# One group of memory values computed right behind the memory keys, the adaptive weights spread over 30 units, and the second norm moved into a 16-unit stage

## The reference

```python
def memory_cross_attention(hn, mem_n, w_q, w_k, w_v, w_o):
    q = (hn @ w_q).reshape(b, s, XA_HEADS, XA_HEAD_DIM)
    k = (mem_n @ w_k).reshape(b, m, XA_HEADS, XA_HEAD_DIM)
    v = (mem_n @ w_v).reshape(b, m, XA_HEADS, XA_HEAD_DIM)
    ...
```

## Time and profile before

| | us |
|---|---|
| median of 3 runs | 3084.89 (3084.48 to 3085.43) |
| time of the profiled execution | 3085.91 |
| its span, first to last instruction | 3084.1 |
| PE busy | 3028.6 |
| DVE busy | 2146.0 |
| ACT busy | 1581.2 |

### The profile page before, as it was taken

The page is one execution under the profiler, slowest core; times in us unless marked ns, Lnnn a source line. Parts: engine busy times, 40 slices in busy tenths (PEclk is TensorE's granted clock), DMA queues, the critical chain, the costliest instruction groups (busy, mean ns, idle before and its releaser), DMA issues.

```text
span 3084.1 us, 44830 instructions
## 1 busy us (share of the span) xinstructions
PE 3028.6 (98%) x16750; PEld 2593.7 (84%) x16750; DVE 2146.0 (70%) x2720; ACT 1581.2 (51%) x1948; POOL 52.2 (2%) x52
## 2 busy tenths in 40 slices
PE   7899999999999999999999999999999999999998
PEld 5688878888788887888888888888888888888887
DVE  3389888788588787647668855566567777777554
ACT  3355444556544566444556654445345555555443
POOL 0032000000000000000000000000000000000000
PEclk9999999999999999999999999999999999999999
DMA  9966848786578656545555555575355555555554
GB/s 392 371 244 232 306 179 314 282 320 228 187 264 294 227 186 219 196 164 197 172 192 168 182 189 191 181 243 197 130 171 178 191 190 190 190 189 188 189 191 143
DMA packets 181403, 667.46 MB, mean 216 GB/s; under 512 B 20212, under 2 KB 20604, under 8 KB 179708
## 3 DMA queue, kind: packets, MB, share of 16 engines
q1 hardware_dynamic: 179580, 661.13, 62.2%
q10 hardware_dynamic: 1664, 4.19, 0.4%
HBM read 658.95 MB, written 6.30 MB: 216 GB/s over the span
## 4 chain that ended last, share of the span: by engine, by line
PE 84%; DVE 8%; DMA 4%; ACT 2%; DVEq 1%; issue 1%; SPq 0%; ACTq 0%
PE acc L791 45%; PE acc L795 22%; PE acc L802 4%; PE acc L804 4%; PE acc L803 4%; DVE w_lo L2060 3%; DMA mod_raw<-in_w_mod 2%; DVE mod_raw L2071 1%; DMA ada_more<-in_w_ada 1%; ACT w_hi L1314 1%; PE msc L839 1%; DMA raw<-in_w_xa_k 1%; PE acc L778 0%; PE msc L1210 0%; PE msc L1230 0%
## 5 line engine op out<-in xcount | busy, mean ns | idle before, releaser
L2060 DVE TENSOR_TENSOR w_lo<-raw,w_hi 128x1024 fp32r<-128x1024 f32 x1020 | 1241.3, 1227 | 597.7 <-ACT w_hi L1314 587.0
L1314 ACT CAST w_hi<-raw 128x1024 fp32r<-128x1024 f32 x1020 | 1061.3, 1048 | 835.6 <-PE acc L795 572.4
L791 PE MATMUL acc<-a_pair,w_hi 128*128 128x512 f32 x2944 | 929.7, 397 | 2.8 <-DVE w_lo L2060 1.6
L795 PEld LDWEIGHTS acc<-a_pair,w_lo 128*128 128x128 f32 x2944 | 553.0, 188 | 130.6
L791 PE MATMUL acc<-b_pair,w_hi 128*128 128x512 f32 x1792 | 569.9, 399 | 18.1 <-DVE w_lo L2060 18.1
L795 PE MATMUL acc<-a_pair,w_lo 128*128 128x256 f32 x2944 | 578.6, 278 | 0.0
L791 PEld LDWEIGHTS acc<-a_pair,w_hi 128*128 128x128 f32 x2944 | 450.3, 189 | 5.1 <-issue 1.9
L791 PE MATMUL acc<-f_pair,w_hi 128*128 128x512 f32 x1408 | 442.4, 395 | 0.0
L795 PEld LDWEIGHTS acc<-b_pair,w_lo 128*128 128x128 f32 x1792 | 337.2, 188 | 79.8
L795 PE MATMUL acc<-b_pair,w_lo 128*128 128x256 f32 x1792 | 352.8, 278 | 0.0
L795 PEld LDWEIGHTS acc<-f_pair,w_lo 128*128 128x128 f32 x1408 | 264.5, 188 | 62.5
(11 more groups left out here) (369 smaller groups left out, 2497.9 us busy)
## 6 DMA issues: line engine op xcount, KB each, us to landing
raw<-in_w_ffn_up SPq DMA_DIRECT2D x176, 512.0 KB, 4.0
mod_raw<-in_w_mod SPq DMA_DIRECT2D x128, 512.0 KB, 5.0
raw<-in_w_ffn_down SPq DMA_DIRECT2D x88, 512.0 KB, 3.3
ada_more<-in_w_ada SPq DMA_DIRECT2D x40, 512.0 KB, 14.2
raw<-in_w_xa_k SPq DMA_DIRECT2D x32, 512.0 KB, 12.6
raw<-in_w_k SPq DMA_DIRECT2D x32, 512.0 KB, 4.5
raw<-in_w_v SPq DMA_DIRECT2D x32, 512.0 KB, 5.6
raw<-in_w_even_out SPq DMA_DIRECT2D x32, 512.0 KB, 4.6
```

Source lines behind the costliest of these rows:

```text
L791: pe.matmul(acc[:, bank(stage, g) + m, :], w_h[:, cols], pair[:, :, kc, :], start=begin, stop=False, skip_group_check=True)
L795: mm = pe.matmul(acc[:, bank(stage, g) + m, 0:T], w_l[:, cols], pair[:, 0, kc, :], start=False, stop=end, skip_group_check=True)
L1314: nc.scalar.copy(w_hi[:, slot], source).then_inc(hi_done, 1)
L2060: vec.tensor_tensor(w_lo[:, slot], source, w_hi[:, slot].bitcast(F32), ALU.subtract).then_inc(lo_done, 1)
```

## The change

It makes the first quarter of the memory's values (8 T units) right behind the keys, so 40 units instead of 32 stand ahead of the context's keys. The modulation's quads are spread over 30 units. The context's load goes behind the last of them, and the context's pair is made at units 33 to 40, one chunk a unit. The second quarter takes the place beside the first norm (same size as before). The stage beside the second norm shrinks from 24 to 16 units, with the norm's steps at earlier units. It also changes some places: `masked` and the scores in `lat_q`, the broadcast load of `top` in two halves, the sums in `even_out`, ACT's step in `SGU_HIGH_AT`; and the second product of a retention head covers only the 128 columns that are read.

```diff
-ADA_OVER = 24
+ADA_OVER = 30
...
     Stage("mem_k", "w_xa_k", "F", 1, groups=4, dve=1),
+    Stage("mem_va", "w_xa_v", "T", 1, groups=1),
     Stage("ctx_k", "w_k", "F", 1, gate=True, act=1, dve=1),
...
     Stage("even_out", "w_even_out", "F", 1, groups=4, act=2, dve=2),
-    Stage("mem_va", "w_xa_v", "T", 1, groups=1),
+    Stage("mem_vb", "w_xa_v", "T", 1, groups=1, first_unit=DC // KU),
     Stage("sgu_v", "w_sgu_v", "T", 1, groups=4, act=1, woven=True),
...
     Stage("odd_out", "w_odd_out", "F", 1, groups=4, act=2, dve=2),
-    Stage("mem_vb", "w_xa_v", "T", 1, groups=3, first_unit=DC // KU),
+    Stage("mem_vc", "w_xa_v", "T", 1, groups=2, first_unit=2 * DC // KU),
     Stage("ret_q", "w_ret_q", "F", 1, act=1, dve=1, woven=True),
...
-          "mlstm_z": spread(16, 14), "pool_z": spread(16, 11), "even_out": range(0, 24, 2), ...
+          "mlstm_z": spread(16, 14), "pool_z": spread(16, 11), "even_out": spread(20, 12), ...
...
-CTX_AT = STAGE["mem_k"].n - 5
-CTX_STEPS = {CTX_AT: (0,), CTX_AT + 1: (1, 2), CTX_AT + 2: (3,), CTX_AT + 3: (4, 5), CTX_AT + 4: (6,)}
-MOD_TURN = CTX_AT - 2
+CTX_AT = STAGE["mem_k"].n + 1
+CTX_STEPS = {CTX_AT + q: (q,) for q in range(7)}
+MOD_TURN = CTX_AT - 1
...
-SGU_HIGH_AT = {at + 1: q for at, q in SGU_NORM_AT.items() if q < 8}
+SGU_HIGH_AT = {at + (1 if q < 2 else 2): q for at, q in SGU_NORM_AT.items() if q < 8}
 SGU_X_AT = {24 + c: c for c in range(DC)}
-MIX_SUMS_AT = 17
-MIX_NORM_AT = 18
-NORMALISE_AT = {4: 0, 6: 1, 8: 2, 10: 3}
-SQUARES_AT = {5: 0, 7: 1, 9: 2, 11: 3}
-MIX_X_AT = {6: 0, 8: 1, 10: 2, 12: 3}
-QUARTERS_AT = {7: 0, 9: 1, 11: 2, 13: 3}
+MIX_SUMS_AT = 12
+MIX_NORM_AT = 13
+NORMALISE_AT = {4: 0, 5: 1, 7: 2, 9: 3}
+SQUARES_AT = {5: 0, 6: 1, 8: 2, 10: 3}
+MIX_X_AT = {7: 0, 9: 1, 11: 2, 13: 3}
+QUARTERS_AT = {6: 0, 8: 1, 10: 2, 11: 3}
...
-SCORES_AT = 13
-MASKED_AT = 14
+SCORES_AT = 12
+MASKED_AT = 11
...
                 def load_key(j):
                     g, k = stage.kinds[j][1:3]
-                    if j == CTX_LOAD_AT:
-
-                        sp.wait_ge(pe_step, BEFORE["mem_norm"]["pe"] + 1)
-                        nc.sync.dma_start(x[:], t["ctx"]).then_inc(ctx_in, 16)
...
+                sp.wait_ge(pe_step, BEFORE["mem_norm"]["pe"] + 1)
+                nc.sync.dma_start(x[:], t["ctx"]).then_inc(ctx_in, 16)
...
-                        if stage.name == "lat_q" and j == 6:
+                        if stage.name == "lat_q" and j in (6, 8):
 
                             sp.wait_ge(top_out, 16)
-                            nc.sync.dma_start(top[:].rearrange("p d h t -> p (d h t)"),
-                                              t["top"].rearrange("d h t -> (d h t)").partition_broadcast(P)).then_inc(top_in, 16)
+                            d = (j - 6) // 2
+                            nc.sync.dma_start(top[:, d].rearrange("p h t -> p (h t)"),
+                                              t["top"][d].rearrange("h t -> (h t)").partition_broadcast(P)).then_inc(top_in, 16)
...
             run("mem_k", b_pair, 0, batch=2, side=mem_sums)
+            run("mem_va", b_pair, PAIR["mem"])
...
-            run("mem_va", a_pair, PAIR["mem_va"], side=first_norm)
+            run("mem_vb", a_pair, PAIR["mem_vb"], side=first_norm)
...
-            run("mem_vb", b_pair, PAIR["mem_vb"], side=second_norm)
-            run("ret_q", a_pair, PAIR["mem_vb"], batch=2)
+            run("mem_vc", b_pair, PAIR["mem_vc"], side=second_norm)
+            run("ret_q", a_pair, PAIR["mem_vc"], batch=2)
...
-                            mm = pe.matmul(msc[:, h % 2, k * T:(k + 1) * T], kf[:, h, k * P:(k + 1) * P], qf[:, h, :],
+                            mm = pe.matmul(msc[:, h % 2, k * T + k * P:(k + 1) * T], kf[:, h, k * P:(k + 1) * P], qf[:, h, k * P:T],
...
             run("mem_k", store_keys, side=mem_chunks)
+            run("mem_va", store_values("mem_va"), side=lambda j: mem_chunks(STAGE["mem_k"].n + j))
...
             run("mem_k", none(), side=mem_chunks, dest=keys_out, scale=token_scale)
+            run("mem_va", none(), side=lambda j: mem_chunks(STAGE["mem_k"].n + j))
```

More of the change, by code:

```diff
@@ L195 @@
           "lat_q": (0, 2, 4, 5, 7, 8, 10, 11, 13), "lat_o": spread(16, 12), "pool_u": spread(16, 9),
-          "mlstm_z": spread(16, 14), "pool_z": spread(16, 11), "even_out": range(0, 24, 2), "sgu_u": spread(32, 18), "sgu_z": spread(26, 14)}
+          "mlstm_z": spread(16, 14), "pool_z": spread(16, 11), "even_out": spread(20, 12), "sgu_u": spread(32, 18), "sgu_z": spread(26, 14)}
 MOD_PLACE = {}
@@ L219 @@
 assert max(MOD_ROWS_AT) < MOD_TURN
-KV_GROUP = {"mem_k": 0, "mem_va": 4, "mem_vb": 5}
+KV_GROUP = {"mem_k": 0, "mem_va": 4, "mem_vb": 5, "mem_vc": 6}
 MEM_AT = [12 + 2 * q for q in range(8)]
@@ L302, in rg_root_step @@
     return rg_act_step(4 * q + 5, 2) + 1 if q < 3 else rg_act_step(DC - 1, 2) + 1
-PAIR = dict(mem=8, ctx=16, lat=24, even_out=28, mem_va=36, sgu=44, odd_out=48, mem_vb=56, mix=64, ret_proj=68, rnn_proj=72,
+PAIR = dict(mem=8, ctx=16, lat=24, even_out=28, mem_vb=36, sgu=44, odd_out=48, mem_vc=56, mix=64, ret_proj=68, rnn_proj=72,
             mix_out=76, xa=84, xa_o=88, ffn=96, ffn_down=107)
@@ L1062, in row_sums @@
                     steps.done(mm)
-            run("sgu_v", b_pair, PAIR["mem_va"], batch=2, side=row_sums)
+            run("sgu_v", b_pair, PAIR["mem_vb"], batch=2, side=row_sums)
             def mix(j):
@@ L1543, in conv_silu, with values, group @@
                 return group
[L1545 to L1552, removed]
+            def values(name):
+                def group(i, g):
+                    first = bank(STAGE[name], g)
+                    for tt in range(2):
+                        mm = nc.scalar.activation(va[:, tt, 2 * g:2 * g + 2, 0:MLSTM_D],
+                                                  acc[:, first + tt, :].rearrange("p (h n) -> p h n", h=2), ACT.Copy, scale=0.5)
+                    mm.then_inc(acc_free, 1)
+                    act.drain()
+                    ran(act.nop())
+                return group
             def wide_and_last(j):
@@ L1589, in key_tokens @@
                     high(j - 9, 1)
-            run("ctx_v", values, side=key_tokens)
+            run("ctx_v", values("ctx_v"), side=key_tokens)
             def first_states(j):
@@ L1616, in exps @@
                     steps.end("lat_gates")
-            run("lat_v", values, side=exps)
+            run("lat_v", values("lat_v"), side=exps)
             def mlstm_exps(r):
@@ L1660, in output_gate @@
             def output_gate(i, g):
-                nc.scalar.activation(both, acc[:, 2 * (g % 2):2 * (g % 2) + 2, :].rearrange("p a b -> p (a b)"), ACT.Tanh,
+                first = bank(STAGE["lat_o"], g)
+                nc.scalar.activation(both, acc[:, first:first + 2, :].rearrange("p a b -> p (a b)"), ACT.Tanh,
                                      scale=0.5).then_inc(acc_free, 1)
@@ L1769, in row_sums @@
             def row_sums(j):
-                sgu_chunks(STAGE["mem_va"].n + j)
+                sgu_chunks(STAGE["mem_vb"].n + j)
                 if j == ROW_SUM_AT:
@@ L1775, in row_sums @@
                                               msc[:, 0:2, :].rearrange("p a b -> p (a b)")))
-            run("mem_va", store_values("mem_va"), side=sgu_chunks)
+            run("mem_vb", store_values("mem_vb"), side=sgu_chunks)
             run("sgu_v", to_tokens("sgu_v", sgu_tok), side=row_sums)
@@ L1825, in mix_chunks @@
                 high_part(a_hi, j - MIX_NORM_AT - 1, "mix_pair")
-            run("mem_vb", store_values("mem_vb"), side=mix_chunks)
+            run("mem_vc", store_values("mem_vc"), side=mix_chunks)
             def halves(slab, g):
@@ L1835, in halves @@
                 dve.add()
-            run("ret_q", lambda i, g: halves(qf, g), side=lambda j: mix_chunks(STAGE["mem_vb"].n + j))
+            run("ret_q", lambda i, g: halves(qf, g), side=lambda j: mix_chunks(STAGE["mem_vc"].n + j))
             run("ret_k", lambda i, g: halves(kf, g))
@@ L2675, in sgu_chunks @@
                     pair_step(b_hi, b_lo, lambda q: normalised(2 * q, 2), SGU_NORM_AT[j], "sgu_pair", first_low_done=True)
-            run("mem_va", none(), side=sgu_chunks)
-            run("sgu_v", none(), side=lambda j: sgu_chunks(STAGE["mem_va"].n + j))
+            run("mem_vb", none(), side=sgu_chunks)
+            run("sgu_v", none(), side=lambda j: sgu_chunks(STAGE["mem_vb"].n + j))
             dve.wait_ge(act_done, ACT_DONE["sgu_v"])
@@ L2787, in mix_chunks @@
                 pair_step(a_hi, a_lo, rms_of(x, "norm_mix"), j - MIX_NORM_AT, "mix_pair")
-            run("mem_vb", none(), side=mix_chunks)
+            run("mem_vc", none(), side=mix_chunks)
             def rotated(slab):
@@ L2800, in rotated @@
                 return group
-            run("ret_q", rotated(qf), side=lambda j: mix_chunks(STAGE["mem_vb"].n + j), dest=in_slab(qf))
+            run("ret_q", rotated(qf), side=lambda j: mix_chunks(STAGE["mem_vc"].n + j), dest=in_slab(qf))
```

5 lines of the change are left out of this document (2 added, 3 removed).

## The result

| | before | after |
|---|---|---|
| median, us (runs) | 3084.89 | 3100.29 (5: 3100.20 to 3102.02) |
| ratio, 95% interval | | 1.0052 [1.0042, 1.0063] |
| profiled span, us | 3084.1 | 3099.0 |
| mean granted clock | 0.997 | 0.993 |

The change makes the kernel slower by 15.4 us; the forecast said slower by 7.2. The value lies inside the forecast's range of 3077 to 3102, close to its upper end, and the likeliest case (slower) is the one that came. It is twice the forecast loss, and 0.3 us beyond the 3084 to 3100 that the prediction gave its forecast case alone. The range reached further only for the rival of the loads, which did not come.

What follows compares the result with a forecast made beforehand. PE, busy 98% of the span, was taken to bound the kernel. Gains of 22.1 us against losses of 21.3 + 8.0 = 29.3 gave net +7.2, so a median of 3092.1 us, range 3077 to 3102.

Steps and rivals of the forecast that it cites:

- the likeliest case (slower): Whole kernel: a median above 3091.1 us, given a chance of 0.42.
- forecast case: Whole kernel: all terms as estimated, median 3092.1 us, 3086 to 3099 (ends of its terms 3084 to 3100); chance 0.52.
- the rival of the loads: Memory's keys: loads still bind and PE keeps stopping, only some 3 of 13.0 us gained, 3102.1 us; chance 0.10.
- the second norm: Stage cut to 16 units: PE waits 8.6 us at column sums, 5.1 + 9.2 in `ret_q`; 21.3 us lost without spells.
- sgu_v: ACT's high part one unit later opens a loop of waits with DVE: 3.7 us gained (0 to 4).
- the heads: Retention heads' scores: narrower second product, 2.0 us gained on PE's path.
- lat_q: Masking and exponentials leave the tail, scores fill a wait: 3.0 us gained (-2 to 3.8).
- The rival in which the norm finds its cover: Second norm: the low part reaches each reader in time, none of 29.3 us lost, 3062.8 us; chance 0.15.
- front: Memory's keys: idle time on `w_ada` and context's pair vanishes, with half-clock spells; 13.0 us gained (3 to 14.3).
- that of the clock: Second norm: stops come but no half-clock spells follow, 3084.1 us, no change; chance 0.23.
- even_out: Modulation sums at new units relieve one wait, may hurt another: 0.4 us gained (-2 to 2).
- The clock: Second norm: five stops of over 3 us, each followed by a 1.6 us half-clock spell: 8.0 us lost (0 to 8.0).

Runs made afterwards that it cites:

- Experiment 1: The changed kernel with the second norm's low part made one unit behind its product instead of two: 3083.66 us, ratio 0.9996.
- Experiment 2: The kernel before with only the edits to `sgu_v`, `lat_q` (with `top` in halves) and the heads: 3077.47 us, ratio 0.9978.
- Experiment 3: `even_out`'s sums: changed kernel with the old units, 3096.91 us; kernel before with the new units, 3089.62 us.
- experiment 6: Changed kernel with low part one unit behind, `even_out`'s sums at old units, and the mask's load in `lat_v` at unit 13 instead of 10: 3077.21 us.
- sums_back: The changed kernel with `even_out`'s sums back at units 0, 2, ... 22: 3096.91 us, ratio 1.0038.
- context_late: The kernel before with only the context's load moved from key unit 23 to 26: 3081.89 us, ratio 0.9989.
- sums_alone: The kernel before with only `even_out`'s twelve sums spread over 20 units: 3089.62 us, ratio 1.0017.
- small_and_late: The kernel before with the edits to `sgu_v`, `lat_q` and the heads, and the context's load at key unit 26: 3073.76 us, ratio 0.9966.

## Why the prediction was right, and where it was short

**Right, and for its reasons: the second norm.** The two ways in which the second norm would be late were forecast from the durations in the earlier trace rows, and came within 0.4 us each: 8.2 for 8.6 at the column sums, 14.5 for 14.3 in `ret_q`. The table's +30.3 stands against +29.3. Experiment 1 shows the mechanism itself, the chunk's low part standing at the unit that reads it. `sgu_v` (-3.8 for -3.7) and the heads (-1.9 for -2.0) were right too. `lat_q` (-3.4 for -3.0) agrees by luck: it was priced from the waits of one execution, and the same code took 2.6 us less in another. Experiment 2 has the three by themselves: 7.0 us between the medians and 9.5 between the profiled spans (3084.1 - 3074.6), where the forecast had 8.7. The rival in which the norm finds its cover is refuted by the stops, that of the loads by a front that gains 11.4 us of its 13.0, and that of the clock by the 9.1 us below.

**The term that failed: `even_out`.** The forecast put it at a gain of 0.4 with bounds of 2 either way, since "sums that leave units 20 and 22 relieve one, those packed closer may hurt another". The measured value is a loss of 3.4, outside these bounds. What the step left out is what DVE has to do at a group's end: two splits are 4.9 us apart there (685.96 and 690.87), more than the 2.78 us of a unit of PE, with the group's own sums and one modulation sum of 1.22 us between them, and a second modulation sum follows. Its lead over PE is used up at that place, and a sum put there is paid in full; the last units, which the change relieves, are one of the three places where PE waited in before (ahead of units 13, 21 and 29), and the waits at the other two grew. A lower clock behind one of them, which the step did not price, is some 1.5 of the 3.4 us. Experiment 3 shows it from both sides.

**The term that was not there: `lat_v`, 2.0 us.** The forecast had no line for a stage in which no edit stands. A wait for a tile of modulation reached PE by way of the gates' scans. Its cause is open (experiment 6).

**The front was 1.6 us short.** Of 12.4 us of idle time behind the kernel's first wait, 3.5 are left, at the last two quads. PE's timeline:

```profile
133.83 1.93 PE L839 MATMUL msc<-ada_more,cond_tile 128*32 128x512 f32 x16 [0.87 <-DMA ada_more<-in_w_ada]
...
141.42 1.92 PE L839 MATMUL msc<-ada_raw,cond_tile 128*32 128x512 f32 x16 [2.66 <-DMA ada_raw<-in_w_ada]
```

The forecast had quad 14's tiles landed at 131.0 and PE there at 133.6, a margin of 2.6 us that it called thin. PE came at 133.0, the tiles at 133.8, which is 5.4 us later than in before and not 2.6. Part of it is that the queue wasn't full all the way. From 40 to 50 us before and then after show (busy per engine, PEclk, DMA share, GB/s):

```profile
40.00:50.00 10.00, 10.00 (x68) 6.12 (x67) 6.72 (x6) 5.00 (x6) 0.00 (x0) 1.00 1.03 409
40.00:50.00 10.00, 10.00 (x64) 7.43 (x63) 4.88 (x6) 3.64 (x4) 0.00 (x0) 1.00 0.98 381
```

From 50 to 75 us it is 410 against 389 GB/s. By these rates the queue of after moved 0.28 + 0.53 MB less by 75 us, which is 1.5 loads or an estimated 2.0 us. From 100 to 125 us it moves 410 GB/s again. The other 0.8 us are open.

Quad 15's wait has a plainer cause, which the forecast's average round of 5.9 loads and 7.1 us hid. With 16 quads over 30 units, quads 14 and 15 stand at neighbouring units, 28 and 29. Between them PE has one quad and one unit, 1.92 + 2.78 = 4.7 us, and the queue four tiles and one unit, 5 x 1.28 = 6.4 us. So PE must stop there for some 1.5 us, and in four other kernels with this spacing it does (1.40 to 1.44 us). After waits 2.66, since its tiles took 7.6 us.

**The clock: 8.0 forecast, 9.1 measured.** The forecast set beside its term a rule that would have made it nought. What the Trainium skill, "TensorE: Matmul & The Clock Gate", section "What's actually happening", states is that the ramp penalty is under 1% of a typical span. The trace agrees with that figure, since 9.1 us are 0.3% of the span; but they are more than half of the whole result, so for this question the term can't be left out. All five stops of 3 us or more were followed by work at the lower level. The page's other statement, that the spells vary, holds: see below. The forecast's own figure of 1.6 for each stop was right for the stops of 5.06 and 3.05 us (the unit behind each takes 1.4 to 1.5 us more than its 2.79). It was low for the one of 8.2 (unit 12 takes 4.9 us against 2.7) and lowest for the last of 3.34, behind which two units take 8.5 us against 5.6. In `sums_back` the same stop of 3.34 us cost 1.7, and that of 5.06 cost 2.5.

The four differences, 1.6 + 2.0 + 3.8 + 1.0, less 0.6 for the rest, are 7.8 us, the distance of forecast (7.2) and spans (14.9) but for rounding. The forecast gave slower the largest chance, 0.42, and its terms for gains were right or too high, none too low by more than 0.4: the terms that it missed lay on one side.

## What to carry to other kernels

When work moves away from beside a chain of another engine, write down for each of the chain's results the unit that produces it and the unit that reads it. Where the two are the same, PE stops once for each; one step index was worth 16.6 to 19.4 us here, more than the 15.4 us that the change lost. Where a load is moved, ask which transfers stand behind it in the same queue at its new place: 2 MB ahead of one quad cost it 4.7 to 4.9 us, whether they stood at unit 23 or at unit 26. And evenly spaced side work is not free in a stage with uneven work of its own: keep it away from the ends of groups.

## What the runs showed of the hardware

The granted clock behind a stop of PE, over all traces of the study. The kernel's first wait of 16 us is left aside, since the profile has no record of the clock before it. Every later idle time of 3.03 us or more (up to 8.25) was followed by work at 0.50. Between 1.77 and 2.70 us it went either way: 1.88 and 2.70 us brought a stretch at 0.50 in before, 1.77 us one in after (`even_out`), 2.37 us one in `context_late`; the 2.66 us of after at quad 15 brought none (the quad takes the usual 1.92 us), nor did its 2.46 us in `even_out` and the 2.22 us of `sums_alone`. The sharpest pair is `context_late` and `small_and_late`, in which PE waits for the same pair at the same place for the same time. The first has, behind its 2.11 us (stretches of 2 us, as above):

```profile
168.00:170.00 2.00, 1.86 (x9) 1.68 (x10) 1.76 (x3) 2.00 (x3) 0.00 (x0) 0.90 0.62 252
170.00:172.00 2.00, 2.00 (x7) 1.63 (x6) 1.82 (x2) 0.19 (x1) 0.00 (x0) 0.50 0.69 213
```

and the second, behind its 2.10 us:

```profile
168.00:170.00 2.00, 1.92 (x10) 1.69 (x11) 1.76 (x3) 2.00 (x3) 0.00 (x0) 1.00 0.48 195
170.00:172.00 2.00, 2.00 (x16) 1.86 (x16) 1.91 (x3) 0.95 (x3) 0.00 (x0) 1.00 0.75 248
```

A stop of about 2 us may thus cost 1 to 2 us more or nothing, from one execution to the next. That may be part of why the same kernel's runs spread over 2 to 7 us here, and a term of this size should be forecast as a range.
